# A two-model transformer chain on one core: a new opening, and the layer norm's root on ScalarE

## The reference

```
for each stage n = 0..9:
    m = stage(x)                       # a mixer or a feed-forward net
    r = ALPHA * x + m                  # ALPHA = 4 ** 0.25
    x = (r - mean(r)) * rsqrt(var(r) + 1e-5) * g[n] + b[n]
```

## Time and profile before

| | |
|---|---|
| median of 3 runs | 1588.84 us (1588.3 to 1589.53) |
| profiled execution | 1589.45 us |
| its span, first to last instruction | 1587.6 us |
| PE busy | 1554.6 us (98%) |
| DVE busy | 1077.0 us (68%) |
| ACT busy | 753.1 us (47%) |
| POOL busy | 18.5 us (1%) |
| mean granted TensorE clock | 0.997 |

### The profile page before, as it was taken

One profiled execution on the slowest core, in us unless ns is written; L12 is line 12 of the kernel. 1 busy time (PEld: TensorE's weight loads), 2 busy tenths in 40 slices (PEclk: granted clock), 3 DMA queues, 4 the chain that ended last, 5 costly groups with the idle time before them and its releaser, 6 DMA issues.

```text
span 1587.6 us, 20708 instructions
## 1 busy us (share of the span) xinstructions
PE 1554.6 (98%) x8570; PEld 1337.1 (84%) x8570; DVE 1077.0 (68%) x1390; ACT 753.1 (47%) x874; POOL 18.5 (1%) x77
## 2 busy tenths in 40 slices
PE   7999999999999999999999999999999999999997
PEld 6978888799888888888888888887888798888886
DVE  6876666768766577655777665577555868965557
ACT  4735444457354443545454354444454365444542
POOL 1000000000000000000000000000000000000000
PEclk9999999999999999999999999999999999999999
DMA  8446565643565556555464655547555462365551
GB/s 265 134 160 212 188 193 176 212 160 114 171 209 197 186 186 209 188 186 187 165 206 133 212 186 189 194 149 239 185 186 188 157 209 95 132 239 185 186 191 48
DMA packets 198444, 285.97 MB, mean 180 GB/s; under 512 B 9287, under 2 KB 167055, under 8 KB 198351
## 3 DMA queue, kind: packets, MB, share of 16 engines
q1 hardware_dynamic: 194943, 272.20, 52.4%
q0 software_dynamic: 3264, 11.93, 2.3%
q10 hardware_dynamic: 144, 0.52, 0.1%
HBM read 283.58 MB, written 1.05 MB: 179 GB/s over the span
## 4 chain that ended last, share of the span: by engine, by line
PE 87%; DVE 9%; ACT 2%; issue 1%; DMA 1%; SPq 0%; DVEq 0%; ACTq 0%
PE ps L397 44%; PE ps L426 25%; PE ps L430 13%; PE ps L449 2%; DVE wlo L293 2%; DVE x L529 1%; DVE res L526 1%; ACT whi L288 1%; DVE stats L503 1%; DVE res L500 1%; DVE xt L488 1%; DMA raw<-in_mla_w_dq 1%; DVE nt L518 1%; PE ps L1574 1%; PE ps L1582 1%
## 5 line engine op out<-in xcount | busy, mean ns | idle before, releaser
L293 DVE TENSOR_TENSOR wlo<-raw,whi 128x2048 fp32r<-128x2048 f32 (+2 forms) x259 | 576.6, 2256 | 227.1 <-ACT whi L288 226.0
L288 ACT ACTIVATE whi<-raw 128x2048 fp32r<-128x2048 f32 (+2 forms) x262 | 483.1, 1879 | 19.6 <-DMA raw<-in_w_in_mlstm 4.7
L397 PE MATMUL ps<-whi,yt 128*128 128x512 f32 (+1 forms) x1472 | 460.9, 386 | 0.5 <-DVE wlo L293 0.5
L426 PE MATMUL ps<-xt,whi 128*128 128x512 f32 x1728 | 431.7, 392 | 0.0
L426 PEld LDWEIGHTS ps<-xt,whi 128*128 128x128 f32 x1728 | 314.2, 189 | 58.6
L397 PEld LDWEIGHTS ps<-whi,yt 128*128 128x128 f32 x1472 | 274.8, 188 | 54.8 <-DVE wlo L293 0.9
L397 PE MATMUL ps<-wlo,yt 128*128 128x512 f32 (+1 forms) x736 | 283.7, 386 | 0.0
L430 PEld LDWEIGHTS ps<-xt,wlo 128*128 128x128 f32 x1728 | 235.7, 190 | 16.9
L430 PE MATMUL ps<-xt,wlo 128*128 128x256 f32 x1728 | 240.9, 282 | 0.0
L397 PE MATMUL ps<-whi,xt 128*128 128x512 f32 (+4 forms) x778 | 222.4, 364 | 3.4 <-DVE wlo L293 2.5
L721 ACT ACTIVATE arena<-ps 128x512 f32<-128x512 f32 x108 | 64.1, 594 | 281.4 <-PE ps L430 281.4
(11 more groups left out here) (229 smaller groups left out, 920.6 us busy)
## 6 DMA issues: line engine op xcount, KB each, us to landing
raw<-in_ffn_w_up SPq DMA_DIRECT2D x76, 1024.0 KB, 5.4
raw<-in_ffn_w_down SPq DMA_DIRECT2D x76, 1024.0 KB, 4.9
raw<-in_ffn_w_gate SPq DMA_DIRECT2D x44, 1024.0 KB, 5.3
raw<-in_diff_w_qkv SPq DMA_DIRECT2D x12, 1024.0 KB, 5.1
raw<-in_w_in_conv SPq DMA_DIRECT2D x10, 1024.0 KB, 5.4
raw<-in_w_out SPq DMA_DIRECT2D x8, 1024.0 KB, 4.9
raw<-in_w_in_mlstm SPq DMA_DIRECT2D x7, 1024.0 KB, 7.3
raw<-in_w_in_mlstm SPq DMA_DIRECT2D x8, 768.0 KB, 4.2
```

What stands on the lines that cost most here:

```text
L288: nc.scalar.activation(whi[:, u.slot, 0:u.size], raw[:, u.slot, 0:u.size], ACT.Copy).then_inc(w_hi[u.slot], 1)
L293: nc.vector.tensor_tensor(wlo[:, u.slot, 0:u.size], raw[:, u.slot, 0:u.size], whi[:, u.slot, 0:u.size].bitcast(F32), ALU.subtract).then_in ...
L397: m = nc.tensor.matmul(out_, p, q, start=first and n == 0, stop=last and n == 2, skip_group_check=True)
L426: nc.tensor.matmul(o.rearrange("p (a n) -> p a n", a=2), parts[c][0], xt2[:, :, c, :], start=c == 0, stop=False, skip_group_check=True)
```

## The change

In the layer norms, for n = 0 to 8: `ln_centre` on DVE only centres and multiplies by the gain. ACT multiplies by the root (`ln_scale`), so that x stands without its offset. PE turns this x, and the offset, now one number per partition and chunk (rows `ln_b0` to `ln_b8` among the parameters), is added as the bias of ACT's copy and as the scalar of DVE's subtraction, with one instruction for each chunk of 128. Tile 1 is turned in four pieces of two chunks, tile 0 in two of four as before. DVE adds the offset to x itself later (`ln_offset`), in the next stage. The last norm is computed as before. ACT splits one weight unit more between the two tiles, and in the last step of a gated net splits the next stage's first units earlier.

In the opening: POOL makes `ident` first, then issues the six small loads, and loads the gains of norm 0 only after the first four units are split. The first weight unit is loaded and split in two halves, right after tile 0 of x. PE runs nine products of zeros before anything else. The turning of the q latents moves into dkv[1], and lambda behind it; DVE's splits of units 4 and 5 move behind the roots and behind lambda.

```diff
+        for n_ in range(N_LN - 1):
+            rows.append((f"ln_b{n_}", layer_norm_params(n_)[1].rearrange("(c p) -> c p", p=P)))
...
+        def load_first(sp, u):
+
+            for k, done in enumerate((first_loaded, w_loaded[u.slot])):
+                sp.dma_start(slot_view(raw, u)[:, 2 * k:2 * k + 2],
+                             u.src[:, 2 * k:2 * k + 2]).then_inc(done, 16)
...
+        def ln_chunks(n, t):
+
+            return HC // 2 if t == 1 and n >= 0 else HC
...
+        def ln_scale(act, n, t, h):
+
+            act.wait_ge(ln_centred, 4 * n + 2 * t + h + 1)
+            half = slice(h * 512, h * 512 + 512)
+            nc.scalar.activation(x[:, t, half], res[:, t, half], ACT.Copy,
+                                 scale=rs[:, t:t + 1]).then_inc(ln_x, 1)
...
+            for p in ln_pieces(n, t, h):
+                act.wait_ge(ln_t, turned(n, t, p))
+                for c in piece_chunks(n, t, p):
+                    m = nc.scalar.activation(xthi[:, c, t * P:(t + 1) * P], turn_view(n, t, p, c),
+                                             ACT.Identity, bias=col(f"ln_b{n}", c))
+                m.then_inc(x_hi, 1)
...
+            for p in ln_pieces(n, t, h):
+                dve.wait_ge(x_hi, turned(n, t, p))
+                for c in piece_chunks(n, t, p):
+                    m = nc.vector.scalar_tensor_tensor(
+                        out=xtlo[:, c, t * P:(t + 1) * P], in0=turn_view(n, t, p, c),
+                        scalar=col(f"ln_b{n}", c), in1=xthi[:, c, t * P:(t + 1) * P].bitcast(F32),
+                        op0=ALU.add, op1=ALU.subtract)
+                m.then_inc(x_lo, 1)
...
-                link(nc.vector.scalar_tensor_tensor(
+                nc.vector.scalar_tensor_tensor(
                     out=res[:, t, half], in0=res[:, t, half], scalar=mv[:, t, 0:1],
-                    in1=gb[:, 0, half], op0=ALU.subtract, op1=ALU.mult))
-                nc.vector.scalar_tensor_tensor(
-                    out=x[:, t, half], in0=res[:, t, half], scalar=y, in1=gb[:, 1, half],
-                    op0=ALU.mult, op1=ALU.add).then_inc(ln_x, 1)
+                    in1=gb[:, 0, half], op0=ALU.subtract, op1=ALU.mult).then_inc(ln_centred, 1)
...
+        def ln_offset(dve, n):
+
+            for t in range(TT):
+                for h in range(2):
+                    half = slice(h * 512, h * 512 + 512)
+                    nc.vector.tensor_tensor(x[:, t, half], x[:, t, half], gb[:, 1, half],
+                                            ALU.add).then_inc(ln_done, 1)
...
-            for t in range(TT if n < N_LN - 1 else 0):
-                for h in range(2):
-                    ln_high(act, n, t, h)
+            if n == N_LN - 1:
+                return
+            ln_scale(act, n, 0, 0)
+            ln_scale(act, n, 0, 1)
+            ln_high(act, n, 0, 0)
+            ln_high(act, n, 0, 1)
+            split.to(upto + 1)
+            for h in range(2):
+                ln_scale(act, n, 1, h)
+                ln_high(act, n, 1, h)
...
+                    if s == f.steps - 1:
+                        split.to(f.tail[0].index + 4)
...
+            split.to(f.head[1].index + 1)
+            ln_offset(dve, FFN_LN[f.k])
             split.to(f.head[1].index + 3)
...
+                            if u is dkv[1] and t == 1 and c == 0:
+                                turn_latents(range(QC), 0)
...
-                    if u is dkv[0]:
+                    if u is dkv[1]:
                         lambda_tensor(pe)
-                        turn_latents(range(QC), 0)
...
-            split.after(dq[0])
             roots(0, QL)
...
-            split.after(dq[1])
+            split.after(dq[0])
             lows(range(QC), (2, 2, 3))
             lambda_vector(dve, link)
+            split.after(dq[1])
             split.after(dkv[0])
             roots(TT, KVL)
...
         def start_gpsimd(pool):
-            load_gb(pool, 0)
-            nc.gpsimd.memset(ident[:, :], 0.0)
+            nc.gpsimd.memset(ident[:, :], 0.0).then_inc(consts, 1)
+            pool.wait_ge(consts, 1)
+            nc.gpsimd.affine_select(out=ident[:, :], in_=ident[:, :], compare_op=ALU.not_equal,
+                                    fill=1.0, base=0, pattern=[[-1, P]],
+                                    channel_multiplier=1).then_inc(consts, 1)
+            start_small_loads(pool)
...
         def start_tensor(pe):
+            pe.wait_ge(idle_made, 1)
+            for _ in range(IDLE_PRODUCTS):
+                nc.tensor.matmul(ps[:, 0, 0:P], idle, idle, start=True, stop=True,
+                                 skip_group_check=True)
...
             start_gpsimd(pool)
+            pool.wait_ge(w_hi[3], 1)
+            load_gb(pool, 0)
```

More of the change, by code:

```diff
@@ new lines, in ln_high @@
+        def ln_high(act, n, t, h):
+            if n < 0:
+                act.wait_ge(ln_t, turned(n, t, h))
+                nc.scalar.activation(half_x(xthi, t, h), half_turned(t, h), ACT.Copy).then_inc(x_hi, 1)
+                return
[5 more added lines that the diff above has]
+                m.then_inc(x_hi, 1)
@@ new lines, in ln_low @@
+        def ln_low(dve, n, t, h):
+            if n < 0:
+                dve.wait_ge(x_hi, turned(n, t, h))
+                nc.vector.tensor_tensor(half_x(xtlo, t, h), half_turned(t, h),
+                                        half_x(xthi, t, h).bitcast(F32),
+                                        ALU.subtract).then_inc(x_lo, 1)
+                return
+            for p in ln_pieces(n, t, h):
+                dve.wait_ge(x_hi, turned(n, t, p))
+                for c in piece_chunks(n, t, p):
+                    m = nc.vector.scalar_tensor_tensor(
[3 more added lines that the diff above has]
+                m.then_inc(x_lo, 1)
@@ L494, in ln_residual, with wait_x @@
+        def wait_x(pe, n, t, c):
+            pe.wait_ge(x_lo, turned(n, t, c // ln_chunks(n, t)))
         def ln_residual(dve, link, n, t, j, last_unit):
@@ L737, in ffn_scalar @@
                         nc.scalar.activation(f_view(0), f_view(2), ACT.Silu).then_inc(f_act, 1)
-                split.to(f.unit["U", s].index + (TAIL if f.gated and s >= f.steps - 2 else 2))
+                split.to(f.unit["U", s].index + (TAIL + (s == f.steps - 1)
+                                                 if f.gated and s >= f.steps - 2 else 2))
                 if f.gated and f.unit["U", s] not in f.head:
                     part("U", s)
+                    if s == f.steps - 1:
+                        split.to(f.tail[0].index + 4)
                 act.wait_ge(f_h, base + s + 1)
@@ L1500, in diff_vector @@
             q, k, v, o = (diff_u[4 * g:4 * g + 4] for g in range(4))
+            split.to(q[3].index)
+            ln_offset(dve, 1)
             for n, group in enumerate((q, k)):
@@ L1743, in token @@
                                         ps[:, c_bank(2), :], ALU.mult).then_inc(c_tok, 1)
+            split.to(conv_u[2].index)
+            ln_offset(dve, 4)
             split.to(conv_u[5].index)
@@ L2166, in ml_vector @@
             link(nc.vector.memset(l_v[:, :, :, MD:], 1.0))
+            split.to(VG[3].index)
+            ln_offset(dve, 7)
             for u in VG[:-1]:
@@ L2275, in build @@
         ang = sb("ang", [P, TT, 3, ROPE // 2 + ROT // 2])
+        idle = arena[:, ARENA - P:]
+        IDLE_PRODUCTS = 9
+        idle_made = sem("idle_made")
         lam_s = sem("lam_s")
@@ L2342, in start_scalar @@
                     ln_high(act, -1, t, h)
-                split.to(0)
+                if t == 0:
+                    first_high(act, order[0], 0)
+                    first_high(act, order[0], 1)
+                    split.n = 1
             split.to(3)
@@ L2352, in start_vector @@
         def start_vector(dve, link, split):
+            nc.vector.memset(idle, 0.0).then_inc(idle_made, 1)
             for t in range(TT):
@@ L2355, in start_vector @@
                     ln_low(dve, -1, t, h)
-                split.to(0)
+                if t == 0:
+                    first_low(dve, order[0], 0)
+                    first_low(dve, order[0], 1)
+                    split.n = 1
             split.to(3)
-            dve.wait_ge(lam_loaded, 64)
+            dve.wait_ge(small_loaded, 16 * SMALL_LOADS)
             l4 = lam_rows[:, :, :].rearrange("p (a b) e -> p a b e", b=2)
@@ L2422, in _ @@
                     start_loads(sp)
-                load(sp, u)
+                if k == 0:
+                    load_first(sp, u)
+                else:
+                    load(sp, u)
             for t in range(TT):
```

107 lines of the change are left out of this document (67 added, 40 removed).

## The result

The changed kernel takes **1604.84 us** (median of 5 runs, 1604.2 to 1608.91) beside 1588.31 for the kernel before (1588.12 to 1589.53): ratio **1.0107** over all runs (the two medians alone give 1.0104), 95% interval 1.0095 to 1.0118. It is slower, by 16.5 us between the medians, where +15.2 was forecast. Its profiled run took 1604.49 us, with a span of 1602.6, 15.0 above the span before.

A forecast was written before the change was run, and what follows sets the result against it. TensorE is busy 98% of the span, so anything adding to its idle time is lost in full. Norms +14.3, clock falls +3.4 and opening -2.5 gave +15.2, 1604 us; range 1588 to 1613, the forecast's own 1595 to 1610.

The forecast's parts named there:

- a: Norms, token tile 0: small offset instructions idle the head 0.7 us to T+2.98 (T: norm's first turn), residual (1,1) 1.5 later.
- b: Norms, root scaled on ACT: chain keeps its length within 0.05; x(1,0) turned at T+8.95 instead of 7.48.
- c: Norm tile 1: x(1,1)'s scaling waits behind ACT's four copies; tile 1 starts T+11.73, +2.2 us at norms 0, 2, 3, 5.
- d: Other norms: norm 1 +2.0, norm 7 +1.7, norms 4 and 6 +0.45 each, norm 8 +0.9; all nine +14.3 us.
- e: Later offset additions on DVE (ln_offset) cost 0; mLSTM head gains, landing about 10 us later, 0, at worst +1.
- f: Opening: first product at 9.9 instead of 14.73, -4.8 us; parameter rows cost 0, at worst +1; slow pace costs as before.
- rival 1: The opening decides and the norms cost little: about -4, 1585 us; 14%.
- g: Opening, lambda wait: DVE splits ahead of kv roots cost +3; latents turned 38.3; opening gives -2.5 us in all.
- h: Granted clock falls behind waits at norms: two falls taken, +3.4 us, bounds 0 and 14.
- rival 2: Norms and opening cancel: norm sum +4 to +6, opening -5, no clock fall, 1589 us; 7%.
- Rival 3: The clock falls at most norms: +24, 1612 us; 11%.

The follow-up runs named there:

- experiment 7: Changed kernel with one copy and one subtraction of 512 columns per half of tile 0, offset left out of the products: 1591.98 us, ratio 1.0023.
- experiment 11: Changed kernel with wide copies and subtractions in both tiles, tile 1's scalings first, offset left out of the products: 1583.1 us, ratio 0.9959.
- experiment 3: Changed kernel with the mLSTM's head gains and gate bias loaded before norm 8's gains and offsets: 1602.79 us, ratio 1.0087.
- Experiment 8: Changed kernel without the nine products of zeros at its start: 1606.77 us, ratio 1.0114.
- experiment 2: The opening-only kernel: kernel before with only the opening changed, norms as before and parameter rows at five loads: 1589.41 us, ratio 1.0003.
- experiment 1: Kernel before with only the norm part of the change, nine more parameter rows in its loads: 1606.13 us, ratio 1.0106.
- experiment 4: Changed kernel with the old latent order: q latents turned and lambda made after the first dkv unit, DVE's splits where they stood: 1605.67 us, ratio 1.0102.
- experiment 5: Changed kernel with ACT's three copies of the q latents before its split of unit 6: 1604.14 us, ratio 1.0097.
- experiment 6: Changed kernel with both of ACT's scalings for token tile 1 before its copies: 1597.16 us, ratio 1.0052.
- experiment 9: Changed kernel with the offsets' parameter rows taken from three arrays in one load each: 1604.94 us, ratio 1.01.
- experiment 12: Norms of the kernel before, with experiment 10's opening, ACT's earlier splits and experiment 3's order of gains: 1583.05 us, ratio 0.9962.
- experiment 10: Changed kernel with rows merged, latent copies and squares ahead of ACT's unit 6 split, DVE's split and norm 0's gains behind the latents: 1601.87 us, ratio 1.008.

## Why the prediction was right

The time came out within 1 us of the forecast, 16.5 above the kernel before where 15.2 was forecast. The mechanism at the norms, a to c, was right and the experiments show it; that the whole came so close is in part luck, as the sum below says. Step by step:

- **a, right.** Forecast: head at T+3.0, residual at T+3.97. Measured T+3.1 and T+3.89, and experiment 7 gives the 1.4 us a norm back. The step of 0.265 holds: (2.18 - 0.37) / 7 = 0.26 on ACT, 0.26 on DVE too. The Trainium skill, "VectorE: DVE Perf Modes", the section on the TRN2 errata, speaks of a fixed latency for each instruction that reads SBUF, and its table has one for PSUM sources too, which these are. The rows agree: a quarter of the columns costs about half the time, 0.26 against 0.49 on ACT (1.09 for two, the last one 0.6) and 0.6 on DVE (1.29 for two). The pointer operand has a part in that 0.26, though. By the rows of experiment 11 the eight small instructions of tile 0 would be shorter without it by some 0.7 us on ACT and 0.5 on DVE; that is an estimate, as no run has small ones without the operand.
- **b, right**, and by experiment 11 the root on ACT is no loss: with wide instructions x(1,1) is turned 0.3 earlier than before. That tile 1 starts 0.6 earlier is half the doing of the pieces of two chunks, which the prediction had called no help; behind the small instructions they were none.
- **c, right** in mechanism: T+11.14 and T+11.56 against 11.27 and 11.73. Turning the order round gave back 0.87 a norm. a and c come from one cause each, and at norms 0, 2, 3 and 5 the 1.4 and the 0.9 that the two repairs give back are more than the +2.0 lost.
- **d, and with it the norms' sum, 2.1 too high**: 12.2 for 14.3. Norms 0, 2, 3 and 5 came out at +2.0, not +2.2, which is 0.8 of it; norms 4 and 6 at +0.04, not +0.45, another 0.8; norms 1, 7 and 8 (+1.9, +1.5 and +0.7 for 2.0, 1.7 and 0.9) make up the rest.
- **e, mis-sized.** "Close to their use: 0, at worst +1" was +2.1, in truth more: 3.7 from norm 7 to norm 8, by experiment 3. The step that failed is "close to their use": I had the 10 us of later issue right and did not read the room that the load had. In the kernel before the bias landed 8.4 us ahead of its use, so 10 us later already means a wait. Measured, the issue comes 10.05 later and the load itself takes 1.5 longer (7.94 for 6.4), which leaves DVE waiting 3.30.
- **f, the first product right** (9.76 for 9.9), two terms wrong. The rows were not free (2.2), and the products of zeros did work: the fast pace from the first product on, which I had given to rival 1. Experiment 8 shows it: without them the first pairs take 0.84 and not 0.51. The Trainium skill, "TensorE: Matmul & The Clock Gate", Part 1, which lets activity release the throttle, agrees. It was worth nearly nothing, 0.5 at norm 0, as the rows were waited for anyway.
- **g, right in kind.** DVE does split from 33.23 to 36.66 ahead of the roots. But the turning of the last kv latents ended at 41.85 and not at 38.3 (41.03 before), for the rows and the q latents' low parts, a wait that the forecast did not have: ACT's split of unit 6 waits until 29.37 for its weights, with the copies queued behind it. The opening cost +0.8 instead of winning 2.5.
- **h, right in size, wrong in place.** Two falls of about 3.4 us (half the pace from 34.0 to 37.4, and around 1318 to 1320), some 1.7 lost in the first and 1.3 in the second (experiment 3): but in the opening and the mLSTM, not at norms. They are inside the +0.8 and the +2.1. And not all of a fall's 1.7 need reach the end: from norm 7's first turn to norm 8's, the kernel before took 129.66 with the fall at norm 7 from which the prediction read its price, and the opening-only kernel 129.40 without one.

So 14.3 + 3.4 - 2.5 was really 12.2 + 0.8 + 2.1. The norms' term carried the forecast. The errors, -2.1 for the norms, -3.4 for the falls at norms, +3.3 for the opening and +2.1 for the mLSTM, cancel to nothing, and that is luck. Of the rivals, 1 falls with the opening's +0.8 and the 0.26 between small instructions, and 2 with the opening. Rival 3 holds for single norms in single runs and never for most: norm 6 in experiment 1, norm 0 in 8, and norm 7 in 4 to 8. What holds the rows up when their offsets come in three loads instead of nine stays open; so does what makes the clock fall in one run and not in the next.

## What to carry to other kernels

On a chain that TensorE waits for, count instructions, and operands read through a pointer, and not elements alone; and ask for each new instruction on an in-order engine what it now stands behind. The two made the norms' 12.2 of the 15.0 us lost. An earlier start is worth only what the next late thing leaves of it. Here single repairs (experiments 4, 5 and 9) gained nothing clear, and four together (rows, copies, splits, gains) kept half of the 5 us; which of the four are needed was not tested. Before a load is issued later, read how long ahead of its use it lands. A tiny one that something waits for goes ahead of the large ones on its queue; where it lands early enough anyway, as in experiment 12, that gives nothing.

## What was not expected of the hardware

The granted clock fell behind some waits of TensorE and not behind others of the same length. Behind the rows it stayed at 1.00 after 2.22 us (changed kernel) and 1.91 (experiment 9), and fell after 2.0 (experiment 3, 0.75 from 15 to 20) and 3.15 (experiment 5). Behind the q latents' low parts 2.45 and 2.72 brought it to 0.57 and 0.50. Behind the first weights, waits of 1.7 and 0.8 us passed without in the changed kernel, and in experiments 2 and 10 waits of about the same length (1.9 and 0.6, 1.7 and 0.8) came with half the clock over the next products. At norm 7 it fell in the kernel before after 1.0 and 0.80, and in the changed kernel not after 1.38 and 1.63; the same two waits came with a fall in experiments 4, 5 and 8. So one profile doesn't say whether a wait costs a fall. And the first products of a run can have the slow pace while the column for the granted clock shows 1.00, as in experiment 8 from 10 to 15 us: at the start, read the pace of the products, not the column.
